# State outputs of an S5 mixer made four tiles at a time on four column tiles of TensorE

## The reference, cut to what matters

```python
bu = jnp.einsum('gpc,bsgc->bsgp', b_bar, ug.astype(jnp.complex64))
a = jnp.broadcast_to(lam_bar, bu.shape)
_, states = lax.associative_scan(_linear_recurrence, (a, bu), axis=1)
y = jnp.einsum('gcp,bsgp->bsgc', c_mat, states).real.reshape(bsz, seq, SSM_WIDTH)
y = y + d_skip.astype(jnp.float32) * uf
y = jax.nn.gelu(y)
y = y * jax.nn.sigmoid(y @ w_glu.astype(jnp.float32))
```

## Time and profile before

| | |
|---|---|
| median of three runs | 2451.28 us |
| the profiled execution | 2438.08 us |
| its span | 2436.0 us |
| first tile's first DVE instruction | 74.18 us |
| last `outputs` matmul ended | 184.1 us |
| product with `w_glu` started | 188.92 us |
| merge, output projection and router | to about 374 us |
| mixture of experts, bound by its weight transfers | from about 374 us |

### The profile page before, as it was taken

One profiled execution on the slowest core, in us unless ns is written; L12 is line 12 of the kernel. 1 busy time (PEld: TensorE's weight loads), 2 busy tenths in 40 slices (PEclk: granted clock), 3 DMA queues, 4 the chain that ended last, 5 costly groups with the idle time before them and its releaser, 6 DMA issues.

```text
span 2436.0 us, 26402 instructions
## 1 busy us (share of the span) xinstructions
PE 2219.9 (91%) x10794; PEld 1294.2 (53%) x10794; DVE 960.1 (39%) x1683; ACT 605.3 (25%) x991; POOL 27.5 (1%) x44
## 2 busy tenths in 40 slices
PE   5888987999999899989975999989998999999998
PEld 3336852333333333333322887557887886555886
DVE  6782132222222222221213554344555553364554
ACT  2103010110101101000102443344444442154443
POOL 0010000000000000000000000000000000100000
PEclk9999989999999999999987999999999999999999
DMA  7534239999999999999996453315443543412541
GB/s 312 207 138 185 109 110 429 426 423 429 428 427 422 427 428 420 427 428 426 423 427 295 156 207 135 130 63 207 172 191 156 194 169 119 162 53 104 207 181 53
DMA packets 40765, 633.64 MB, mean 260 GB/s; under 512 B 4800, under 2 KB 4800, under 8 KB 5728
## 3 DMA queue, kind: packets, MB, share of 16 engines
q1 hardware_dynamic: 40640, 631.90, 63.0%
HBM read 630.84 MB, written 1.05 MB: 259 GB/s over the span
## 4 chain that ended last, share of the span: by engine, by line
PE 68%; DMA 18%; DVE 4%; ACT 2%; issue 1%; SPq 0%; ACTq 0%; DVEq 0%
DMA piece<-in_moe 18%; PE bank L1768 10%; PE bank L1684 10%; PE bank L1686 10%; PE bank L1685 9%; PE bank L599 6%; PE bank L1803 5%; PE bank L1218 3%; PE bank L1181 2%; PE bank L1749 2%; PE bank L1827 2%; PE bank L1185 1%; PE bank L1013 1%; DVE ffn_lo L1690 1%; PE bank L1022 1%
## 5 line engine op out<-in xcount | busy, mean ns | idle before, releaser
L1768 PE MATMUL bank<-piece,xeT 128*64 128x512 f32 (+1 forms) x2304 | 454.3, 632 | 74.2 <-DMA piece<-in_moe 71.5
L1690 DVE TENSOR_TENSOR ffn_lo<-slot,ffn_hi 128x2048 fp32r<-128x2048 f32 x132 | 302.1, 2292 | 175.6 <-ACT ffn_hi L2193 169.9
L1768 PEld LDWEIGHTS bank<-piece,xeT 128*64 128x64 f32 (+1 forms) x2304 | 135.7, 133 | 359.8 <-issue 335.1
L1684 PE MATMUL bank<-ffn_hi,hT_hi 128*128 128x512 f32 x704 | 280.5, 398 | 8.4 <-DVE hT_lo L523 6.0
L2193 ACT ACTIVATE ffn_hi<-slot 128x2048 fp32r<-128x2048 f32 x132 | 251.8, 1913 | 139.5 <-PE bank L1686 124.5
L1686 PE MATMUL bank<-ffn_hi,hT_lo 128*128 128x512 f32 x704 | 275.5, 391 | 0.0
L1685 PE MATMUL bank<-ffn_lo,hT_hi 128*128 128x512 f32 x704 | 274.8, 390 | 0.0
L1875 DVE TENSOR_TENSOR hT<-hT,bank 128x512 f32<-128x512 f32 x144 | 92.2, 682 | 268.9 <-PE bank L1827 262.2
L599 PE MATMUL bank<-slot,hT 128*128 128x512 f32 (+1 forms) x384 | 170.6, 595 | 0.0
L1922 DVE TENSOR_SCALAR work<-bank 128x256 f32<-128x256 f32 x60 | 25.5, 425 | 360.0 <-PE bank L1775 360.0
L1684 PE MATMUL bank<-ffn_hi,act_hi 128*128 128x512 f32 x352 | 141.2, 401 | 18.6 <-DVE act_lo L1690 18.6
(11 more groups left out here) (602 smaller groups left out, 2292.4 us busy)
## 6 DMA issues: line engine op xcount, KB each, us to landing
piece<-in_moe SPq DMA_DIRECT2D x192, 2048.0 KB, 25.9
slot<-in_ffn SPq DMA_DIRECT2D x44, 3072.0 KB, 10.2
slot<-in_ada SPq DMA_DIRECT2D x6, 3072.0 KB, 10.1
slot<-in_merge SPq DMA_DIRECT2D x4, 3072.0 KB, 13.8
slot<-in_nsa_in SPq DMA_DIRECT2D x5, 2048.0 KB, 7.6
slot<-in_w_in SPq DMA_DIRECT2D x4, 2048.0 KB, 8.9
slot<-in_ada SPq DMA_DIRECT2D x3, 2560.0 KB, 8.9
slot<-in_hy_in SPq DMA_DIRECT2D x3, 2048.0 KB, 7.9
```

Of the source, the lines that this page charges most:

```text
L1684: pe.matmul(out, left[0], right[0], start=start, stop=False)
L1690: return dve.tensor_tensor(lo, x, hi.bitcast(F32), ALU.subtract)
L1768: pe.matmul(bank[n * c:n * (c + 1), :], x[:, kt, :], w[i][:, at:at + 512], start=kt == 0, stop=False)
```

## The change

`outputs` now takes a quad: its 16 matmuls go round the four column tiles, so four neighbours in the list have different columns of the array, different PSUM partitions and different R. It stands at steps 4, 8 and 12, behind the work put between, for the quad that ended one tile before, and once behind the loop. R of six tiles is kept instead of two: two in `ssm_r`, four in the last 2048 numbers of slots 1 and 2. `ssm_y_ready` counts quads. The transfer merge1, which overwrites slot 1, waits for the last quad's outputs instead of the last tile's inputs.

```diff
-    item("ssm_b", ("ssm_b", 0), 4096, (sig["bu_ready"], SSM_TILES), slot=1)
+    item("ssm_b", ("ssm_b", 0), 4096, (sig["ssm_y_ready"], SSM_TILES // SSM_Q), slot=1)
...
+def ssm_rows(k, j):
+    i = j % SSM_ROWS
+    if i < 2:
+        return k["ssm_r"][:, i, :, :, :]
+    at = 4096 + 1024 * (i % 2)
+    return k["ring"][i // 2][:, at:at + 1024].rearrange("p (a b c) -> p a b c", a=2, b=2)
...
-        if j >= 2:
-            dve.wait_ge(s["ssm_y_ready"], j - 1)
-        R = k["ssm_r"][:, j % 2, :, :, :]
+        if j >= SSM_ROWS:
+            dve.wait_ge(s["ssm_y_ready"], (j - SSM_ROWS) // SSM_Q + 1)
+        R = ssm_rows(k, j)
...
-    dve.wait_ge(s["ssm_y_ready"], 4 * q + 4)
+    dve.wait_ge(s["ssm_y_ready"], q + 1)
...
-    def outputs(j):
-        q, jj = divmod(j, SSM_Q)
-        if jj == 0 and q >= 2:
+    def outputs(q):
+        if q >= 2:
             pe.wait_ge(s["gelu_in"], q - 1)
-        if j == 0:
+        if q == 0:
             pe.wait_ge(s["gcol_done"], 1)
             pe.wait_ge(s["ssm_prep_dve"], 2)
-        pe.wait_ge(s["rotated"], j + 1)
-        out = k["ps"][6 + q % 2][32 * jj:32 * jj + 32, 0:S]
-        R = k["ssm_r"][:, j % 2, :, :, :]
-
+        pe.wait_ge(s["rotated"], SSM_Q * (q + 1))
         for n_, (c, trig, part) in enumerate(((0, 0, 0), (1, 1, 1), (2, 0, 1), (2, 1, 0))):
-            mm = pe.matmul(out, k["c_mix"][:, c, 32 * j:32 * j + 32], R[:, trig, part, :], start=n_ == 0, stop=n_ == 3)
+            for jj in range(SSM_Q):
+                j = SSM_Q * q + jj
+                mm = pe.matmul(k["ps"][6 + q % 2][32 * jj:32 * jj + 32, 0:S], k["c_mix"][:, c, 32 * j:32 * j + 32], ssm_rows(k, j)[:, trig, part, :], start=n_ == 0, stop=n_ == 3)
         mm.then_inc(s["ssm_y_ready"], 1)
...
-        outputs(j)
+        if j >= SSM_Q and j % SSM_Q == 0:
+            outputs(j // SSM_Q - 1)
+    outputs(SSM_TILES // SSM_Q - 1)
```

More of the change, by code:

```diff
@@ L63 @@
 SSM_Q = 4
+SSM_ROWS = 6
 HEADS, HD = 8, 64
```

## The result

The ratio of the changed kernel to the one before, from 11 runs of each, is 0.9949, with a 95% interval of 0.9934 to 0.9965. On 2451.28 us that is 12.5 us saved, between 8.6 and 16.2. The medians are 2435.68 and 2446.57 us, 10.9 apart: over eleven runs the kernel before has a lower median than over the three that the forecast started from. So the kernel is faster by about half a per cent. The forecast ratio was 2438.8 / 2451.28 = 0.9949, and that is what was measured.

What follows compares the result with a forecast made beforehand. It took the tight PE-DVE relay, its end set by PE, as the bound. Stage end 184.1 to 171.0 gives 13.1, less 0.5 for a broadcast and 0.1 for the tight place: 12.5 off 2451.28, 2438.8 us, range 2425.4 to 2446.

Steps and rivals of the forecast that it cites:

- DVE becomes the bound: In the stage, DVE's waits on `inputs` and conditioning product fall from 14.9 to under 2 us; 10.5 to 14.5 saved.
- The quad's price: PE's 32 `outputs` records for four tiles take 1.86 us, the last quad 3.5 at the low clock.
- Rival C: In the quads, column tiles load weights one after the other: 11.5 us a quad, slower, 2445.6 us; chance 0.06.
- The 22 us: PE's `outputs` work falls from 29.4 us at best for 16 tiles to 7.4 for four quads.
- The clock at the end: PE's 5.6 us gap before the last quad halves the clock: 3.5 us instead of 1.86.
- The tight place: Steps 3 to 5, where slot 0 takes conditioning weights one by one; 0.1 us taken off the saving.
- 0.9 us of cover: At step 5 PE ends the conditioning product at 103.6 us, before DVE arrives at 104.5.
- rival A: Cover at step 5 or the clock gives way; saves 5 to 10 us, centre 8 (2430); chance 0.2.
- rival A's first part: First conditioning product at the low clock takes 2.8 us more; 1.9 of that is beyond the cover.
- A DVE wait behind tile 5: Sign in DVE's list that the forecast is wrong and rival A holds.
- forecast case: DVE becomes the stage's bound, 10.5 to 14.5 us saved; chance 0.65.
- Rival C's variant without overlap: Quads with loads hidden but no overlap take 7.4 us; stage ends at about 181, 3 us saved.

Runs made afterwards that it cites:

- warm_gap: Changed kernel plus five unused 512-column matmuls in PE's gap before the last quad; stage 98.0 us against 99.7, one run.
- rows_shift: Kernel before with six R kept and `outputs` one step later, one tile at a time; ratio to before 0.9954, stage 98.3 us.
- shift_two: Kernel before with only `outputs` one step later, still two R, one tile at a time; ratio to before 0.9963, stage 99.9 us.
- serial_quad: Changed kernel with each quad's matmuls ordered tile by tile instead of round the column tiles; ratio to before 0.9969, stage 105.9 us.
- wides_early: Changed kernel with the four last broadcasts of conditioning rows moved ahead of the last quad's outputs; ratio to before 0.9931.
- wides_row_late: wides_early with DVE's first conditioning row one tile later, behind tile 6 instead of tile 5; ratio to before 0.9912.
- shift_wides: rows_shift with the last four broadcasts ahead of tile 15's outputs; stage 104.7 us, one run.
- rows_only: Kernel before with six R kept instead of two, `outputs` where they were; `w_glu` product at 116.32 us from the first tile (before 114.74), one run.

## Why the prediction was right, and where not

**DVE becomes the bound: right, but less fully than forecast.** Its waits on `inputs` and the conditioning product fell from 14.9 to 2.2 us, and the chain runs over DVE up to the last R. Several signs that the prediction set for itself were missed by a little: the waits ("under 2"), the last R at 168.78 (167 to 168.5) and the product at 177.51 (176 to 177), the last two although this execution started its first tile 1.3 us earlier. Counted from the first tile, the last R was forecast at 93.0 to 93.4 and came at 95.90: the 2.2 us of waits are most of that.

**The quad's price: right.** 1.86 forecast, 1.93 measured; 3.5 and 3.64 at the low clock. By the rule of the Trainium skill (TensorE: Matmul & The Clock Gate, Part 3) loads of other column tiles don't hide behind running matmuls, and a quad would take 2.75 us by my estimate. The trace disagrees for 256 columns too: 1.93. Rival C falls with it. The 22 us that the sum took out of PE's work came to 25.3 (34.7 to 9.4). The clock at the end fell because of the gap, as assumed; warm_gap shows it.

**The tight place: too little taken off.** I took off 0.1 us. PE in order of time, steps 2 to 5, and then DVE at the row:

```profile
84.59 1.13 PE L864 MATMUL bank<-uT,slot 128*128 128x256 f32 x4 [1.78 <-DVE work L819]
89.13 5.31 PE L304 MATMUL bank<-slot,cond 128*32 128x512 f32 x24 [3.42 <-DMA slot<-in_ada]
...
103.51 1.92 PE L304 MATMUL bank<-slot,cond 128*32 128x512 f32 x16
```

```profile
105.50 0.69 DVE L315 TENSOR_TENSOR work<-bank,slot 128x512 f32<-128x512 f32 x1 [1.92 <-PE bank L304]
```

With `outputs` gone from steps 1 to 3, PE ran dry for 3.42 us before the conditioning weights landed, and the product ran at 0.52 of the clock, 2.53 us longer than the 2.78 that the sum took; the weights themselves took 11.0 us to land instead of 10.1. DVE waited 1.92 us for the next product. Where 0.9 us of cover was forecast there was none. DVE had waited 1.90 us at this same row before the change, so here nothing was gained at all; what vanished is the 3.53 us at the second row, and nearly all of the 9.5 on `inputs`.

This is the mechanism of rival A's first part and the 1.9 us that it named, but at another product: A put the low clock at the first one, which ran at 1.00 here, and it came at the one behind it. A DVE wait behind tile 5 was also one of the prediction's own signs of being wrong. I had held against A that a gap of 1.97 us left the clock up; this gap is longer. From 89.13 on PE has no idle time ahead of the product at 103.51, so by estimate a product of 2.78 us at step 3 would have brought the later one 2.53 us forward, more than DVE's 1.92. No run tests the clock apart. In rows_shift the product of step 3 ran at 1.00 and DVE still waited 0.90 us at this row, with more `outputs` work in PE's list.

**The size: that it agrees is luck.** In the profile the product moved by 10.1 us (114.74 to 104.63), not 12.5: the difference is the 2.2 us of waits and small things. At the experts' start 9.1 remain. Both lie below the 10.5 to 14.5 that the prediction gave its forecast case, near the upper end of rival A's 5 to 10. The ratio's 12.5 us has an interval of 8.6 to 16.2 and holds either, the medians say 10.9; so that the ratio equals the forecast doesn't show the sum to be right. The last 1 us may be nothing: from the product to the experts' start the eleven executions took between 183.5 and 186.7 us, whatever the kernel (185.7 before, 186.7 now).

**The reason given for it: wrong in one step.** The sum argued that PE loses 22 us of work and therefore keeps up. The row that spoke against it was in my own hand: 12.6 us of PE waiting for R, in the same 110 us in which DVE waited 14.9 us for PE. Where both wait for each other, the order of the list may be what is wrong, and here it was. shift_two takes no work from PE and saves 10.1 us at the product, 9.1 by its ratio. The change moved `outputs` behind a later step and also made them cheap, and I credited the second. The place of `outputs` was no term of the sum and no rival. The later place alone accounts for all of the changed kernel's gain that these runs can resolve; the column tiles pay for what bunching in quads costs (serial_quad) and leave a gap at the end that only wides_early turns into time. Rival C's variant without overlap had a wrong price too: the serial quad takes 4.59 and not 7.4 us, and saves 4.0 at the product (3 by the forecast).

What stays open: why the clock in the later layers' attention differs between executions, why the first conditioning product ran at the full clock in some and not in others, and whether the low clock at step 3 is all of the 1.92 us.

## What to carry to other kernels

When two engines of a relay both show waits for each other, first move the consumer's matmuls one step later in the list, behind the instruction that the other engine wants next; two buffers may suffice, as in shift_two. Only then ask whether making them cheaper matters: it does where the room it makes is filled with work from the end, as the four broadcasts here (5.4 us at the mark; the ratios, 0.9931 against 0.9949, have intervals that overlap). And with a scatter of 0.5% between executions, compare marks inside the stage, counted from its start, not spans.

## What the hardware showed

- Four column tiles of 32 columns, fp32, 256 moving columns: 32 records in 1.93 us, 64 in 3.66. One tile alone takes 1.84 for 8. Side by side they run 3.8 times as fast.
- Tile after tile, 32 records still take 4.59 us, not 7.4; two tiles in rows_shift took 2.81 us, not 3.7:

```profile
169.25 2.81 PE L879 MATMUL bank<-slot,c_mix 128*32 128x256 f32 x16
```

- TensorE's clock behind a gap, read at conditioning products of 24 records (2.78 us at 1.00). Gaps of 3.42 us (changed kernel), 4.46 (serial_quad) and 5.20 (wides_row_late) were followed by 5.31, 5.30 and 5.08 us. Near 2 us both happened: 1.97 and 2.16 (shift_wides) were followed by 2.78 us at 1.00, 2.11 (rows_only) by 4.36 at 0.63 and 2.13 (wides_early, at 117.25) by 4.48 at 0.62. So at that length the gap alone doesn't tell.
- The last quad took 1.94 us at 1.00 behind a gap of 0.39 us, and 3.64 at 0.50 behind one of 5.16.
- The later layers took 1097.5 to 1108.5 us with the same code, with the granted clock in two of their stretches at 0.99 or 0.95.
